# The last of four pairs of feature tiles of each post-sublayer norm on GpSimd instead of VectorE, in a decoder trunk

## The chip, the cores and the metric

The kernel runs on one core of a Trainium2 chip. The metric is device time in microseconds (us) of one execution. Engines are named as the profile names them: PE is TensorE's matmuls, PEld its loads of weights, DVE is VectorE, ACT ScalarE, POOL GpSimd, SP the engine that issues most DMAs.

## What is computed

One inference step of a trunk of four layers, for a prompt of 256 tokens and 8 samples of one token that share all weights (264 columns together, 1024 features, float32). Layer i has a token mixer (sparse attention, gated recurrence, state-space scan, sparse attention again) and then a squared-ReLU MLP. Around every sublayer stands the same frame:

```python
# Every sub-layer: x <- x + gate(c) * RMSNorm_post(f(RMSNorm_pre(x) * (1 + scale(c)) + shift(c)))
def _rmsnorm(x, g):
    x32 = x.astype(jnp.float32)
    y = x32 * lax.rsqrt(jnp.mean(x32 * x32, axis=-1, keepdims=True) + NORM_EPS)
    return (y * g.astype(jnp.float32)).astype(x.dtype)
...
        xp = xp + gtp_m * _rmsnorm(mp, norm_gains[i, 1])
        hp = _rmsnorm(xp, norm_gains[i, 2]) * (1.0 + scp_f) + shp_f
        xp = xp + gtp_f * _rmsnorm(_sq_relu_mlp(hp, w_mlp_in[i], w_mlp_out[i]), norm_gains[i, 3])
```

## The kernel before

Activations lie feature-major: `xT` (the residual x), `mT` (a sublayer's output) and `hT` (its input) are 128 partitions x 8 tiles of features x 264 columns. A program for each engine is written by hand, with semaphores between them; a `Signal` counts what was given on one. Weights stream through a ring of four slots by SP. Nothing in the order is left to a scheduler: what stands in the code of an engine is its order.

`stage_trunk(l, ...)` is one block of instructions for each layer l: the output projection of the mixer, the norm behind it, the norm ahead of the MLP, the MLP, the norm behind that, and the norm ahead of layer l+1's mixer with its first part (or, in the last layer, the transposes to the output). Two sets of norm signals, s0 and s1, serve the two halves. So `post_dve` and what follows it run eight times: four times with s0, behind a mixer, and four times with s1, behind an MLP.

At each of the eight places the work goes like this. The output's squares are added up over the features on PE by a multiplication with ones (`sum_m`, L419, or L617 in the MLP), and ACT makes the root of it in two steps (`rms_act`, L427 and L428), which writes `rstd`. Meanwhile DVE multiplies `mT` by gain times gate (`coef_post`): the prompt's columns tile by tile (L440), the samples' in one operation (L441). Then, with `rstd`, DVE multiplies pairs of tiles by the root (L446, in place) and adds them to x (L455), four pairs, each of 2 tiles x 264 = 528 columns; the multiplication of the next pair stands ahead of the addition of this one. Each addition gives `x_done`.

Then comes the norm ahead of the next sublayer. ACT squares each tile as soon as its pair of x is done (`pre_act`, L494 and L495), PE adds the squares up (`rms_pe`, L413), ACT makes the root again (L427, L428). DVE in the meantime prepares `coef_pre` (L463, L464), waits for the last `x_done`, multiplies the samples' columns (L468) and, ahead of an MLP only, makes two of the four mixed blocks of the MLP's first weights (`early`: L702, L705). Then it multiplies x by the root into `hT` (L474), after which ACT (L501) and DVE (L485) scale and shift, and the next sublayer's matmuls start. While PE has nothing to do, it multiplies ones by ones (`keep_clock`, L406): seven times ahead of the squares and six behind them. In the last layer PE transposes x instead (L831), each pair as its `x_done` comes, DVE copies the results from PSUM (L840), four tiles at a time, and SP writes the output.

The first stage (`stage_first`) loads tables of parameters by DMA on ACT's queue, and PE transposes them (L3133) when `tables_in` has counted 13 of them; two more loads, `relb` and `nar` (narrow constants, L3166 and L3167), count on a semaphore of their own, `narrow_in`, that the matmul behind the transposes (L3136) waits for. GpSimd has no work in this kernel but four fills at its start; it takes part in the barriers between blocks.

Of the kernel before, what the change touches and what calls it, by code (L numbers as in the profile page):

```python
# [16 lines left out]
ALU = mybir.AluOpType  # L17
# [144 lines left out]
def hybrid_trunk(nc, a, outs, consts, stop=None):  # L162
# [3 lines left out]
    with ctx:  # L166
# [11 lines left out]
        xT = sb("xT", [128, DT, T])  # L178
        hT = sb("hT", [128, DT, T])
        mT = sb("mT", [128, DT, T])  # L180
# [72 lines left out]
        taken = signal("taken")  # L253
        fetched = [signal(f"fetched{i}") for i in range(4)]
        ada_loaded = [signal(f"ada_loaded{j}") for j in range(3)]
        ada_ready = signal("ada_ready")
# [14 lines left out]
        class NormSignals:  # L271

            def __init__(self, n):
                self.m_squared = signal(f"m_squared{n}")
                self.m_moved = signal(f"m_moved{n}")
                self.m_summed = signal(f"m_summed{n}")
                self.m_rstd = signal(f"m_rstd{n}")
                self.x_done = signal(f"x_done{n}")
                self.x_squared = signal(f"x_squared{n}")
                self.x_summed = signal(f"x_summed{n}")  # L280
                self.x_rstd = signal(f"x_rstd{n}")
                self.x_scaled = signal(f"x_scaled{n}")
                self.h_sample = signal(f"h_sample{n}")
                self.h_act = signal(f"h_act{n}")
                self.h_dve = signal(f"h_dve{n}")
# [137 lines left out]
        def rms_act(act, summed, done, bank):  # L423
# [4 lines left out]
            done.on(nc.scalar.activation(rstd[:, :], rstd[:, :], ACT.Exp, scale=-0.5))  # L428

        def post_dve(v, s, l, which, moved=None):  # L430

# [6 lines left out]
            for t, ready, k in moved or [(t, s.m_moved, 5 + t) for t in range(DT)]:  # L438
                v.wait_ge(ready.sem, ready.at(k))
                nc.vector.tensor_scalar_mul(mT[:, t, 0:SEQ], mT[:, t, 0:SEQ], coef_post[:, t, 0:1])  # L440
            step(nc.vector.tensor_tensor(mT[:, :, SEQ:T], mT[:, :, SEQ:T], coef_post[:, :, 1:C], ALU.mult))  # L441
            v.wait_ge(s.m_rstd.sem, s.m_rstd.at(1))

# [5 lines left out]
            scale(0)  # L449
            for p in range(4):  # L450
                if p < 3:
                    scale(p + 1)
                v.wait_ge(dve_step.sem, dve_step.at(first + p + 1))
                x = xT[:, 2 * p:2 * p + 2, :]
                s.x_done.on(nc.vector.tensor_tensor(x, x, mT[:, 2 * p:2 * p + 2, :], ALU.add))  # L455

        def pre_dve(v, s, l, which, after_post, early=None):
# [7 lines left out]
            if after_post:  # L465
                v.wait_ge(s.x_done.sem, s.x_done.at(4))
            samples = hT[:, :, SEQ:T]
# [20 lines left out]
        def pre_act(act, s, l, which, bank, after_post):  # L488


            for p in range(4):
                if after_post:
                    act.wait_ge(s.x_done.sem, s.x_done.at(p + 1))
                s.x_squared.on(nc.scalar.activation(sq[:, 2 * p, :], xT[:, 2 * p, :], ACT.Square))  # L494
                s.x_squared.on(nc.scalar.activation(sq[:, 2 * p + 1, :], xT[:, 2 * p + 1, :], ACT.Square))  # L495
# [323 lines left out]
        def output_parts(s):  # L819
            ytok = Place(8448 + 12288)(3, D)  # L820

            def pe_part(pe):
                for i in range(3):
                    n = 128 if i < 2 else NB
                    for h in range(2):
                        if i:
                            pe.wait_ge(mm_taken.sem, mm_taken.at(2 * i + h - 1))
                        for t in range(4):
                            if i == 0:
                                pe.wait_ge(s.x_done.sem, s.x_done.at(2 * h + t // 2 + 1))  # L830
                            ins = nc.tensor.transpose(PS[0:n, h, t * 128:(t + 1) * 128],  # L831
                                                      xT[:, 4 * h + t, i * 128:i * 128 + n], ident)
                        mm_ready.on(ins)
# [1270 lines left out]
        def mixer_nsa(l, h):  # L2104
# [7 lines left out]
            return parts, rest  # L2112

        logs, aux_made, copied = signal("logs"), signal("aux_made"), signal("copied")

# [948 lines left out]
        c_in, x_in, wide_in = signal("c_in"), signal("x_in"), signal("wide_in")  # L3064
        tables_in, narrow_in = signal("tables_in"), signal("narrow_in")
        coef_ready, bounds_raised = signal("coef_ready"), signal("bounds_raised")

        def stage_first():
# [30 lines left out]
            with nc.Block() as block:  # L3099
# [13 lines left out]
                def _(pe):  # L3113
# [15 lines left out]
                    rms_pe(pe, s1.x_squared, s1.x_summed, 3)  # L3129
                    pe.wait_ge(tables_in.sem, tables_in.at(16 * 13))  # L3130
                    for n, (i, r, o) in enumerate(spans):
                        pe.wait_ge(mm_taken.sem, mm_taken.at(9 if n < 4 else n + 6))
                        mm_ready.on(nc.tensor.transpose(PS[:, 4 + n % 4, 0:r], rows[0:r, i, :], ident[0:r, 0:r]))  # L3133
                    pe.wait_ge(narrow_in.sem, narrow_in.at(32))
                    o, n = NARROW_AT["by_dist"]
# [26 lines left out]
                def _(act):  # L3162
                    step = stepper(act, act_step)
                    for src, i, r, n in tables:
                        tables_in.on(act.dma_start(rows[r:r + n, i, :], src), 16)
                    narrow_in.on(act.dma_start(relb, a["rel_bias"]), 16)  # L3166
                    narrow_in.on(act.dma_start(nar, consts[1][:, 0:4352]), 16)  # L3167
                    for j, name in enumerate(("ssd_dt_bias", "ssd_a_log", "ssd_d")):
# [90 lines left out]
        def stage_trunk(l, source, mixer):  # L3259
# [10 lines left out]
            with nc.Block() as block:  # L3270
                @block.sync
                def _(sp):
                    proj_sp(sp)
                    mlp_sp(sp)
                    next_sp(sp)

                @block.tensor
                def _(pe):
# [68 lines left out]
```

## Time and profile before

| | |
|---|---|
| median of 3 runs | 2615.28 us (2610.3 to 2617.28) |
| the profiled execution, its own time | 2611.51 us |
| its span, first to last instruction | 2609.7 us |
| mean granted clock of TensorE | 0.934 |
| PE busy | 2445.3 us, 94% |
| PEld busy | 2071.7 us, 79% |
| DVE busy | 1322.4 us, 51% |
| ACT busy | 740.4 us, 28% |
| POOL busy | 0.2 us |

All rows below are from this one execution; times are us from the start of its span. PE's matmuls are pipelined and the ends of their rows are modelled. A row of the timeline may merge several instructions of one kind that follow each other (x2, x8); the number in its brackets is how long the engine had been idle before it, with what ended the idle time.

### The profile page before, as it was taken

Reading aid. Unit: us, or ns where it says so; the run is one execution under the profiler, and the core shown is the slowest. Engines: PE = TensorE matmul, PEld = TensorE weight load, DVE = VectorE, ACT = ScalarE, POOL = GpSimd, SP = SyncE. Lnnn points to the kernel's source line nnn. Section 1 sums busy time; section 2 is a strip of 40 time slices with the busy share of each in tenths; the row PEclk is TensorE's granted clock in tenths of the full one; section 3 lists DMA queues with packets and bytes.
Section 4 is the critical chain, followed back from the end, with each engine's and each line's share of the span. In section 5 each row is a group of like instructions: output and inputs, shape, how many; then the busy total and the mean of one; then the engine's idle time right before and its main releaser. Section 6 shows DMA issues by size and latency. Waiting matters only on the chain. (4 is left out here: it accounts for less than half of the span.)

```text
span 2609.7 us, 45644 instructions
## 1 busy us (share of the span) xinstructions
PE 2445.3 (94%) x19266; PEld 2071.7 (79%) x19266; DVE 1322.4 (51%) x2361; ACT 740.4 (28%) x1781; POOL 0.2 (0%) x4
## 2 busy tenths in 40 slices
PE   8989988999999888999999896999999899989998
PEld 6668865699986766999888664899985787648998
DVE  2257374366542464555443395165540874535665
ACT  1125373211022342210232393121011454522200
POOL 0000000000000000000000000000000000000000
PEclk8999798999999978999999856999999997889999
DMA  9997617867633325676333252666653875093440
GB/s 345 289 247 162 207 41 222 294 227 268 250 129 129 97 73 193 237 278 240 131 129 131 66 162 73 217 255 247 252 179 79 178 202 156 27 322 137 168 176 30
DMA packets 287344, 472.73 MB, mean 181 GB/s; under 512 B 14956, under 2 KB 105149, under 8 KB 286662
## 3 DMA queue, kind: packets, MB, share of 16 engines
q1 hardware_dynamic: 272370, 456.04, 53.6%
q10 hardware_dynamic: 14770, 13.76, 1.7%
q8 instruction: 153, 2.51, 0.4%
q14 instruction: 51, 0.42, 0.0%
HBM read 448.72 MB, written 38.04 MB: 187 GB/s over the span
## 5 line engine op out<-in xcount | busy, mean ns | idle before, releaser
L598 PE MATMUL PS<-hT,ring 128*128 128x132 f32 x2048 | 250.3, 277 | 6.1 <-DVE hT L723 4.2
L598 PEld LDWEIGHTS PS<-hT,ring 128*128 128x128 f32 x2048 | 238.3, 190 | 12.6 <-issue 11.8
L598 PE MATMUL PS<-mT,arena 128*128 128x132 f32 x1536 | 185.3, 276 | 0.0
L598 PEld LDWEIGHTS PS<-mT,arena 128*128 128x128 f32 x1536 | 179.1, 190 | 0.0
L2624 PE MATMUL PS<-hT,ring 128*128 128x264 f32 x768 | 172.7, 386 | 0.3 <-DVE hT L480 0.3
L2624 PEld LDWEIGHTS PS<-hT,ring 128*128 128x128 f32 x768 | 145.1, 190 | 25.1 <-issue 0.6
L735 DVE TENSOR_TENSOR arena<-arena,PS 128x264 f32<-128x264 f32 x224 | 89.7, 427 | 129.4 <-PE PS L598 128.3
L682 ACT ACTIVATE arena<-arena 128x528 f32<-128x528 f32 x64 | 41.1, 642 | 311.8 <-DVE arena L735 311.8
L1443 DVE COPY arena<-PS 64x512 f32<-64x512 f32 (+1 forms) x160 | 94.2, 588 | 68.8 <-PE PS L1317 67.7
L598 PE MATMUL PS<-arena,ring 128*128 128x132 f32 x1024 | 127.5, 278 | 0.0
L598 PE MATMUL PS<-mT,ring 128*128 128x132 f32 x1024 | 125.7, 276 | 0.0
L598 PE MATMUL PS<-hT,arena 128*128 128x132 f32 x1024 | 125.7, 276 | 0.0
L598 PEld LDWEIGHTS PS<-arena,ring 128*128 128x128 f32 x1024 | 120.1, 190 | 3.6 <-issue 3.6
L598 PEld LDWEIGHTS PS<-hT,arena 128*128 128x128 f32 x1024 | 120.5, 190 | 0.3
L598 PEld LDWEIGHTS PS<-mT,ring 128*128 128x128 f32 x1024 | 120.2, 190 | 0.0
L1462 ACT ACTIVATE arena<-PS 64x512 f32<-64x512 f32 (+1 forms) x160 | 82.9, 518 | 125.3 <-PE PS L1317 124.3
L2077 PE MATMUL PS<-hT,ring 128*128 128x264 f32 x384 | 92.1, 396 | 13.4 <-PEq L2524 9.9
L687 ACT ACTIVATE hT<-PS 128x264 f32<-128x264 f32 x8 | 3.1, 390 | 351.2 <-PE PS L598 351.2
L2077 PEld LDWEIGHTS PS<-hT,ring 128*128 128x128 f32 x384 | 74.8, 195 | 27.4 <-issue 14.2
L440 DVE TENSOR_SCALAR mT<-mT,coef_post 128x256 f32<-128x256 f32 x64 | 20.1, 351 | 150.8 <-ACT mT L394 150.7
L2139 PE MATMUL PS<-hT,ring 128*128 128x264 f32 x384 | 85.9, 386 | 0.3 <-DVE hT L480 0.3
L1051 PE MATMUL PS<-ring,hT 128*128 128x512 f32 x192 | 84.7, 596 | 1.3 <-DMA ring<-in_nsa_w_in 1.3
(473 smaller groups left out, 4423.4 us busy)
## 6 DMA issues: line engine op xcount, KB each, us to landing
arena<-in_w_ada SPq DMA_DIRECT2D x36, 2048.0 KB, 12.1
ring<-in_w_mlp_in SPq DMA_DIRECT2D x32, 2048.0 KB, 8.6
ring<-in_w_mlp_out SPq DMA_DIRECT2D x32, 2048.0 KB, 8.4
ring<-in_w_ada SPq DMA_DIRECT2D x12, 2048.0 KB, 16.8
ring<-in_ssd_w_in SPq DMA_DIRECT2D x12, 2048.0 KB, 8.0
ring<-in_nsa_w_in SPq DMA_DIRECT2D x10, 2048.0 KB, 9.4
arena<-in_cache_nsa_kv SPq DMA_DIRECT2D x64, 256.0 KB, 11.1
ring<-in_cache_nsa_kv SPq DMA_DIRECT2D x64, 256.0 KB, 7.7
```

Of the source, the lines that this page charges most:

```text
L440: nc.vector.tensor_scalar_mul(mT[:, t, 0:SEQ], mT[:, t, 0:SEQ], coef_post[:, t, 0:1])
L598: ins = nc.tensor.matmul(PS[:, bank, at:at + HALF], lhs[:, k, p * 128:(p + 1) * 128], rhs[:, k, :], start=opens and k == 0, stop=closes an ...
L682: step(nc.scalar.activation(x, x, ACT.Relu))
L687: mlp_copied.on(nc.scalar.activation(n1, both(0), ACT.Copy))
L735: mlp_sums.on(nc.vector.tensor_tensor(dst, x, y, ALU.add))
L1051: ins = nc.tensor.matmul(PS[:, n % 4, :], hT[:, k, m * 128:(m + 1) * 128], w[:, k, :], start=k == 0, stop=k == 7)
L1443: ins = nc.vector.tensor_copy(dst, src)
L1462: ins = nc.scalar.activation(dst, src, ACT.Copy)
L2077: ins = nc.tensor.matmul(PS[:, 4 * h + m, 0:T], w[:, k, m * 128:(m + 1) * 128], src[:, 8 * d + k, :], start=d == 0 and k == 0, stop=d == d ...
L2139: ins = nc.tensor.matmul(PS[:, n % 4, 0:T], w[:, k, m * 128:(m + 1) * 128], hT[:, k, :], start=k == 0, stop=k == 7)
L2624: ins = nc.tensor.matmul(PS[:, n % 4, 0:T], w[:, k, m * 128:(m + 1) * 128], hT[:, k, :], start=k == 0, stop=k == 7)
```

## The change

In each of the eight places the fourth pair of tiles (tiles 6 and 7) of `mT` is multiplied by the root and added to x by GpSimd, in a new function `post_pool`; VectorE does the first three pairs. GpSimd waits for a new semaphore, `m_weighted`, that VectorE raises when the weights of the samples are in, and for the root; between its two instructions it waits for the first. What waited for the fourth `x_done` now waits for `x_done_pool`: ScalarE's squares of tiles 6 and 7, VectorE's L468, and PE's transposes of tiles 6 and 7 at the end. To have the three semaphores for this, two of `fetched`, one of `ada_loaded` and `narrow_in` go; the two loads of `narrow_in` are counted on `tables_in`, so that the transposes of the parameter tables wait for them too.

```diff
-        fetched = [signal(f"fetched{i}") for i in range(4)]
-        ada_loaded = [signal(f"ada_loaded{j}") for j in range(3)]
+        fetched = [signal(f"fetched{i}") for i in range(2)]
+        ada_loaded = [signal(f"ada_loaded{j}") for j in range(2)]
...
+                self.x_done_pool = signal(f"x_done_pool{n}")
...
+        def post_pool(gp, s, n):
+
+
+            m, x = mT[:, 6:8, :], xT[:, 6:8, :]
+            gp.wait_ge(m_weighted.sem, m_weighted.at(n + 1))
+            gp.wait_ge(s.m_rstd.sem, s.m_rstd.at(1))
+            pool_step.on(nc.gpsimd.tensor_tensor(m, m, bc(rstd[:, :], 1, 2), ALU.mult))
+            gp.wait_ge(pool_step.sem, pool_step.at(n + 1))
+            s.x_done_pool.on(nc.gpsimd.tensor_tensor(x, x, m, ALU.add))
+
         def post_dve(v, s, l, which, moved=None):
...
             step(nc.vector.tensor_tensor(mT[:, :, SEQ:T], mT[:, :, SEQ:T], coef_post[:, :, 1:C], ALU.mult))
+            v.sem_inc(m_weighted.sem, 1)
+            m_weighted.given += 1
             v.wait_ge(s.m_rstd.sem, s.m_rstd.at(1))
...
-            for p in range(4):
-                if p < 3:
+            for p in range(3):
+                if p < 2:
                     scale(p + 1)
...
             if after_post:
-                v.wait_ge(s.x_done.sem, s.x_done.at(4))
+                v.wait_ge(s.x_done.sem, s.x_done.at(3))
+                v.wait_ge(s.x_done_pool.sem, s.x_done_pool.at(1))
...
             for p in range(4):
-                if after_post:
+                if after_post and p < 3:
                     act.wait_ge(s.x_done.sem, s.x_done.at(p + 1))
+                elif after_post:
+                    act.wait_ge(s.x_done_pool.sem, s.x_done_pool.at(1))
...
-                            if i == 0:
+                            if i == 0 and 4 * h + t < 6:
                                 pe.wait_ge(s.x_done.sem, s.x_done.at(2 * h + t // 2 + 1))
+                            elif i == 0:
+                                pe.wait_ge(s.x_done_pool.sem, s.x_done_pool.at(1))
...
-                    pe.wait_ge(tables_in.sem, tables_in.at(16 * 13))
+                    pe.wait_ge(tables_in.sem, tables_in.at(16 * 15))
...
-                    pe.wait_ge(narrow_in.sem, narrow_in.at(32))
...
-                    narrow_in.on(act.dma_start(relb, a["rel_bias"]), 16)
-                    narrow_in.on(act.dma_start(nar, consts[1][:, 0:4352]), 16)
+                    tables_in.on(act.dma_start(relb, a["rel_bias"]), 16)
+                    tables_in.on(act.dma_start(nar, consts[1][:, 0:4352]), 16)
...
+                @block.gpsimd
+                def _(gp):
+                    post_pool(gp, s0, 0)
+                    post_pool(gp, s1, 1)
```

DVE's instructions behind the mixer of layer 0, before, from the weights of the samples to the first multiplication into `hT` (in brackets the semaphores waited for):

```order
L441 TENSOR_TENSOR mT<-mT,coef_post 128x8x8
L446 TENSOR_TENSOR mT<-mT,rstd 128x528 [waits m_rstd0,dve_step]
L446 TENSOR_TENSOR mT<-mT,rstd 128x528
L455 TENSOR_TENSOR xT<-xT,mT 128x528 [waits dve_step]
L446 TENSOR_TENSOR mT<-mT,rstd 128x528
L455 TENSOR_TENSOR xT<-xT,mT 128x528 [waits dve_step]
L446 TENSOR_TENSOR mT<-mT,rstd 128x528
L455 TENSOR_TENSOR xT<-xT,mT 128x528 [waits dve_step] x2
L463 TENSOR_SCALAR coef_pre<-mod 128x72
L464 TENSOR_TENSOR coef_pre<-coef_pre,par 128x72 [waits dve_step]
L468 TENSOR_TENSOR hT<-xT,coef_pre 128x8x8 [waits x_done0,dve_step]
```

The same stretch on DVE after the change (line numbers are those of the changed kernel):

```order
L452 TENSOR_TENSOR mT<-mT,coef_post 128x8x8
L459 TENSOR_TENSOR mT<-mT,rstd 128x528 [waits dve_step,m_rstd0]
L459 TENSOR_TENSOR mT<-mT,rstd 128x528
L468 TENSOR_TENSOR xT<-xT,mT 128x528 [waits dve_step]
L459 TENSOR_TENSOR mT<-mT,rstd 128x528
L468 TENSOR_TENSOR xT<-xT,mT 128x528 [waits dve_step] x2
L476 TENSOR_SCALAR coef_pre<-mod 128x72
L477 TENSOR_TENSOR coef_pre<-coef_pre,par 128x72 [waits dve_step]
L482 TENSOR_TENSOR hT<-xT,coef_pre 128x8x8 [waits x_done_pool0,x_done0,dve_step]
```

One multiplication and one addition are gone from the row, and the samples' operation waits for GpSimd too. GpSimd, which had no rows here, has in each layer's block:

```order
L437 TENSOR_TENSOR mT<-mT,rstd 128x528 [waits m_rstd0,m_weighted]
L439 TENSOR_TENSOR xT<-xT,mT 128x528 [waits pool_step]
L437 TENSOR_TENSOR mT<-mT,rstd 128x528 [waits m_rstd1,m_weighted]
L439 TENSOR_TENSOR xT<-xT,mT 128x528 [waits pool_step]
L3288 UNCONDITIONAL_BRANCH
```

The first two stand behind the mixer, the next two behind the MLP; the second pair waits in the queue for most of the block.

## Rows read from the trace of the kernel before

**Rows 1.** The page: busy time by engine (share, instructions), and the chain's shares.

```profile
PE 2445.3 (94%) x19266; PEld 2071.7 (79%) x19266; DVE 1322.4 (51%) x2361; ACT 740.4 (28%) x1781; POOL 0.2 (0%) x4
...
PE 9%; DVE 1%; ACT 0%; issue 0%; DVEq 0%
```

**Rows 2.** One line, L446: duration ns min/median/max, first and last start, form.

```profile
L446 DVE TENSOR_TENSOR mT<-mT,rstd x32: 698/702/710, 505.6 to 2598.1; 128x528 f32<-128x528 f32 x32
```

**Rows 3.** Timeline, middle place of layer 0: start, length, engine, line, operation [idle before].

```profile
505.55 1.33 DVE L446 TENSOR_TENSOR mT<-mT,rstd 128x528 f32<-128x528 f32 x2 [1.04 <-ACT rstd L428]
506.80 0.70 DVE L455 TENSOR_TENSOR xT<-xT,mT 128x528 f32<-128x528 f32 x1
...
508.03 0.70 DVE L455 TENSOR_TENSOR xT<-xT,mT 128x528 f32<-128x528 f32 x1
508.65 0.70 DVE L446 TENSOR_TENSOR mT<-mT,rstd 128x528 f32<-128x528 f32 x1
...
509.25 0.74 PEld L413 LDWEIGHTS PS<-arena,ones 128*128 128x128 f32 x4 [0.49 <-ACT arena L494]
509.27 1.32 DVE L455 TENSOR_TENSOR xT<-xT,mT 128x528 f32<-128x528 f32 x2
510.01 0.42 ACT L494 ACTIVATE arena<-xT 128x264 f32<-128x264 f32 x1 [0.50 <-DVE xT L455]
...
510.48 1.63 PEld L413 LDWEIGHTS PS<-arena,ones 128*128 128x128 f32 x8 [0.50 <-ACT arena L494]
...
511.00 0.22 DVE L468 TENSOR_TENSOR hT<-xT,coef_pre 128x64 f32<-128x64 f32 x1
...
512.52 1.23 DVE L705 TENSOR_TENSOR ring<-ring 128x1024 f32<-128x1024 f32 x1
...
513.08 0.42 ACT L428 ACTIVATE rstd<-rstd 128x264 f32<-128x264 f32 x1
513.66 0.69 DVE L474 TENSOR_TENSOR hT<-xT,rstd 128x512 f32<-128x512 f32 x1
```

**Rows 4.** L474: idle time before it by releaser (us, times); then one mixer place.

```profile
L474 DVE TENSOR_TENSOR hT<-xT,rstd x28: 682/686/694, 513.7 to 2386.7; 128x512 f32<-128x512 f32 x28
...
  ACT rstd L428: 7.1, 3
...
758.56 0.69 DVE L474 TENSOR_TENSOR hT<-xT,rstd 128x512 f32<-128x512 f32 x1 [2.38 <-ACT rstd L428]
```

**Rows 5.** Timeline at the end of the program, behind the last MLP.

```profile
2595.01 1.33 DVE L446 TENSOR_TENSOR mT<-mT,rstd 128x528 f32<-128x528 f32 x2 [0.24 <-ACT rstd L428]
...
2598.11 0.70 DVE L446 TENSOR_TENSOR mT<-mT,rstd 128x528 f32<-128x528 f32 x1
...
2598.73 1.32 DVE L455 TENSOR_TENSOR xT<-xT,mT 128x528 f32<-128x528 f32 x2
...
2599.96 1.31 DVE L840 COPY arena<-PS 128x512 f32<-128x512 f32 x2
2600.10 0.20 PEld L831 LDWEIGHTS PS<-wide,xT 128*128 128x128 f32 x2 [0.42 <-DVE xT L455]
```

**Rows 6.** Timeline: GpSimd's work, first of its four fills.

```profile
0.24 0.10 POOL L3332 MEMSET const-float32-0.0<- 128x1 f32 x1 [0.24 <-issue]
```

**Rows 7.** First stage: issue of the narrow table, the transposes; DMA issues with us to landing.

```profile
6.30 0.44 ACTq L3167 DMA_DIRECT2D arena<-const_narrow  x1
...
21.17 0.56 PEld L3133 LDWEIGHTS PS<-wide,arena 128*128 128x128 f32 x4
...
arena<-const_narrow ACTq DMA_DIRECT2D x1, 544.0 KB, 8.2
```

**Rows 8.** Busy us (count) by engine in stretches; PEclk is the granted clock.

```profile
core 0: us, PE busy (x) PEld busy (x) DVE busy (x) ACT busy (x) POOL busy (x), PEclk, DMA share, GB/s
...
507.50:512.40 4.90, 4.23 (x17) 3.01 (x18) 4.80 (x9) 2.84 (x8) 0.00 (x0) 1.00 1.05 405
...
2595.70:2599.10 3.40, 1.70 (x8) 0.78 (x6) 3.40 (x7) 0.00 (x0) 0.00 (x0) 1.00 0.01 2
2599.10:2602.50 3.40, 2.67 (x14) 1.70 (x15) 2.88 (x6) 0.00 (x0) 0.00 (x0) 0.80 0.00 0
```

More of the change, by code:

```diff
@@ L2112, in mixer_nsa @@
             return parts, rest
+        m_weighted = signal("m_weighted")
         logs, aux_made, copied = signal("logs"), signal("aux_made"), signal("copied")
@@ L3064, in hybrid_trunk @@
         c_in, x_in, wide_in = signal("c_in"), signal("x_in"), signal("wide_in")
-        tables_in, narrow_in = signal("tables_in"), signal("narrow_in")
+        tables_in = signal("tables_in")
         coef_ready, bounds_raised = signal("coef_ready"), signal("bounds_raised")
```

## The prediction, made before the change was run

> **What bounds the kernel now.** I read the page's busy shares first, then the chain that ended last, then the stretch around one norm in order of time. TensorE is busy 94% of the span, VectorE 51%, GpSimd not at all, and the chain that ended last lies almost wholly on TensorE [rows 1]. So a change on VectorE counts only where TensorE has nothing else to do. Those places are the norms behind a sublayer: x may not be multiplied again before it is scaled, added, squared, summed, scaled again and shifted. There are eight of them: 32 multiplications by the root of 0.702 us, four at a place [rows 2]. Four are "middle" places (behind a mixer, ahead of the MLP), three are "mixer" places (behind an MLP, ahead of the next mixer), and one is the end (ahead of the output).
>
> The middle place of layer 0 [rows 3]. VectorE starts the first multiplication at 505.55 and then runs eight operations of one pitch, 509.27 - 508.65 = 0.62 us, each 0.70 us long. Call them S0 S1 A0 S2 A1 S3 A2 A3 (S multiplies a pair by the root, A adds it to x). ScalarE squares each pair when its A ends: the third from 510.01. TensorE adds up the squares: eight loads of weights for the last four tiles from 510.48, 1.63 us, so 0.41 us a tile without a gap. From the third pair on it is TensorE's own pace, not VectorE, that sets when the sum is there: the chain runs through A2, not through A3. Then come the second root (its end 513.08 + 0.42 = 513.50) and VectorE's L474 at 513.66. In a middle place VectorE has its own chain beside it: L468 at 511.00, two preparations of weights, the last from 512.52 for 1.23 us, so until 513.75. That is as late as the root. L474 waited for the root at three places only, the mixer places, with 2.38 us idle [rows 4].
>
> **What the change does to each part.**
>
> 1. S3 and A3 leave VectorE: 2 x 0.62 us at each of eight places. If nothing else is touched, A2 starts at 508.65 instead of 509.27. Its pair could be squared 0.62 us earlier, but TensorE began the second pair's two tiles at 509.25 [rows 3] and needs 0.82 us for them, so the third pair starts at 510.07 instead of 510.48: **0.41 us gained** on the sum. In a middle place VectorE's own chain ends 1.24 us earlier, at 512.51, ahead of the root at 513.09; L474 gains 0.41 and the 0.05 us by which it followed the root later there than at a mixer place. Seven places: 7 x 0.41 + 4 x 0.05 = 3.1 us. At the end of the program the last pair is transposed from 2600.10 and the copy that waited for it followed [rows 5]. With A2 ended 0.62 us earlier, tiles 4 to 7 need 0.88 us from 2598.86: done 2599.74 instead of 2600.54, of which VectorE's copies leave 0.6. Sum: **-3.7 us**.
>
> 2. GpSimd makes the pair: two operations of 128x528 at each place, in its own queue with nothing behind them. Behind its results wait ScalarE (squares of the last pair, and behind them the root and the shifts), VectorE (L468 and behind it the two preparations and L474), and at the end TensorE. No row shows GpSimd computing at this width; it has four fills of one column, 0.10 us each [rows 6]. Bounds: 0.70 us (VectorE's own price) and 1.4 us, twice that. I take 1.25 us, near VectorE's 1.23 us for 1024 columns [rows 3], since an engine without a second fast reader would read the two inputs of 528 columns one behind the other. By the Trainium skill, "GPSIMD Engine Reference", section "Elementwise — side-by-side cycle accounting", it is 1.96 times VectorE's time at 2048 columns; by that alone it would be an estimated 1.38 us. No run here shows it yet. Undisturbed, the pair is ready at 505.55 + 0.1 + 2 x 1.25 + 0.1 = 508.25. It is needed for a square that must be done when TensorE reaches tile 6 (510.07 + 0.82 = 510.89), so from about 510.45: over 2 us to spare. Each operation could last 2.3 us and still cost nothing.
>
> 3. The new wait and the semaphore. VectorE adds one to a semaphore behind L441 (the samples' weights). Its idle time ahead of S0 is 1.04 us at a middle place [rows 3] and 0.24 us at the others [rows 5], of which 0.13 lies before the root is there. Cost 0 to 0.1 us at four places; I take 0.
>
> 4. The merged wait in the first stage. The transposes of the parameter rows, from 21.17 us, now also wait for the table of narrow constants. It was issued at 6.30 and landed 8.2 us later, at 14.5 [rows 7]. The cover is the sum of squares ahead of the transposes; 6.7 us to spare. Cost 0. The three semaphores taken away are waited for nowhere.
>
> **What the two engines do to each other** is the term that decides. Every one of VectorE's six remaining operations reads two tensors of SBUF, and so do both of GpSimd's; all start from the same root at the same moment. ScalarE squares x beside VectorE's additions and neither is longer for it: all 32 multiplications lie between 698 and 710 ns [rows 2]. That speaks for free running, but shows ScalarE, not GpSimd. If the two share a way to SBUF and an operation holds it to its end, the work of both is in line: 6 x 0.62 + 2 x 1.25 = 6.2 us where eight operations took 4.96. Who goes first decides what it costs.
>
> - In turns: S0, GpSimd, S1, GpSimd, A0, S2, A1, A2. A1 ends at 511.23, A2 at 511.85 (before: 508.73, 509.97). TensorE starts the second pair 0.52 us behind A1, at 511.75, and the third at 512.57 instead of 510.48: **+2.1 us**. At the end A2 ends at 2601.31 and 0.9 us of transposes follow: +1.7. Sum 7 x 2.1 + 1.7 = **+16.4 us**.
> - VectorE first, since its next operation stands ready when one ends: A2 is 0.62 us early, GpSimd starts at 509.27 and its pair is done at 511.9. Tile 6 is summed from 512.35 instead of 511.30: +1.05 at a mixer place, about +1.0 at a middle one (VectorE's chain, held at L468, ends 514.7), +1.3 at the end. Sum 4.0 + 3.1 + 1.3 = **+8.4 us**.
>
> With GpSimd at 0.70 us the two are +7.6 and about 0, with 1.4 us +18.5 and +10.5.
>
> I forecast that they are in line, between the two orders: **+12.4 us**. The reason is the place more than the price: each pair of GpSimd operations meets a row of VectorE operations without a gap [rows 3], so any exclusion, whichever engine wins, falls on the chain. The skill has a rule that speaks against this change: "SBUF — State Buffer", section "Who interferes with whom", says a VectorE instruction with two SBUF inputs contends with a GpSimd instruction that reads SBUF, the second blocking until the first is finished. By it the two sums above hold, without it the -3.7; no row here shows it yet.
>
> **The rivals.**
>
> - *Free running.* GpSimd and VectorE don't disturb each other, or only GpSimd is longer and stays inside its 2 us to spare. Then -3.7 us. For it: ScalarE beside VectorE, and the wide margin. Against it: no row has GpSimd in it. Time 2615.3 - 3.7 = 2611.6.
> - *The clock falls too.* With the turns, TensorE is empty from 507.5 to 510.5, between its filling multiplications and the first square; today it is 4.23 of 4.90 us busy there at a granted clock of 1.00. At the end of the program a stretch of 3.4 us in which it was busy 1.70 us is followed by one with a mean of 0.80, part of it at 1.2 GHz instead of 2.4 [rows 8]. At 0.80 over 3.4 us 1.4 us are at half speed, 0.7 lost; at most 1.7 us if all is. Seven places: 5 to 12 us on top of 16.4, so some +25 us: 2640.
>
> **How the numbers follow.** The sums are against the profiled execution (span 2609.7, its time 2611.5); the median of the three runs is 3.8 us higher, and the same differences are put on it: 2615.3 + 12.4 = 2627.7, rounded to **2627.5 us**. Chances: in line 0.52, free running 0.38, clock too 0.08, something else 0.02. A measurement of this kernel tells about 0.3%, 7.8 us, from no change. No case gains that much: faster 0.02. Slower: most of the first case (0.44; the rest has a quick GpSimd or VectorE going first), the clock and half of the unknown, 0.54. Within 0.3%: 0.44. The range reaches from the free case less 3 us of spread, 2608, to the turns with GpSimd at 1.4 us and the same spread, 2637; beyond it lies mainly the clock case.
>
> **What would show it.** Right: at eight places GpSimd operations over 1.3 us long or starting only when a VectorE operation ends, VectorE operations with pitches of 1.8 us in the row S0 to A2, L474 one to two us later after S0 than the 8.11 us of today. Free running: the six operations at pitches of 0.62, GpSimd done before A2, the third pair's sum 0.4 us earlier. Clock: a granted clock under 1.00 in the 13 us behind a place. The forecast is wrong above all if reading two tensors on both engines is no conflict, or if GpSimd's stretch of waiting fits into its own 2 us.

## The result

The changed kernel takes 2640.77 us (median of 4 runs, 2637.74 to 2643.12), the kernel before 2612.84 (4 runs, 2610.3 to 2617.28): a ratio of 1.010, interval 1.0084 to 1.0115, so **slower by 22 to 30 us**. Measured twice more, it was 1.0071 (1.0049 to 1.0093) and 1.0101 (1.0082 to 1.0119). The sign is the forecast's, and so is the cause, two engines in line; the size is not. 2640.8 lies above the range's 2637, and where I wrote 12.4 us it was about 20 at the eight places alone. One of the six runs of the kernel called *idle pair beside* below took 6151.68 us and is in no time or ratio given here.

The page of the changed kernel, busy shares and the chain, as [rows 1] of before:

```profile
PE 2453.3 (93%) x19266; PEld 2080.0 (79%) x19266; DVE 1331.2 (50%) x2345; ACT 740.1 (28%) x1781; POOL 27.4 (1%) x20
...
PE 9%; DVE 1%; ACT 0%; issue 0%
```

VectorE has 16 instructions fewer (2361 to 2345) and yet is busy for 9 us longer. The groups by line say which (us busy and mean ns of one; line 459 is 446 of before, 468 is 455):

```profile
L459 DVE TENSOR_TENSOR mT<-mT,rstd 128x528 f32<-128x528 f32 x24 | 25.0, 1070 | 4.5 <-ACT rstd L429 4.5
...
L468 DVE TENSOR_TENSOR xT<-xT,mT 128x528 f32<-128x528 f32 x24 | 24.9, 1062 | 0.0
```

```profile
L437 POOL TENSOR_TENSOR mT<-mT,rstd 128x528 f32<-128x528 f32 x8 | 14.0, 1755 | 2600.3 <-ACT rstd L429 2600.3
L439 POOL TENSOR_TENSOR xT<-xT,mT 128x528 f32<-128x528 f32 x8 | 13.1, 1639 | 0.6
```

Where a multiplication by the root had a mean of 0.702 us [rows 2], it now has 1.07. That is no general slowness. The timeline of the first place, which answers to [rows 3], shows it to be two operations at each place (start, length, engine, line, operation, idle time before):

```profile
512.39 2.43 DVE L459 TENSOR_TENSOR mT<-mT,rstd 128x528 f32<-128x528 f32 x2 [0.97 <-ACT rstd L429]
512.51 1.75 POOL L437 TENSOR_TENSOR mT<-mT,rstd 128x528 f32<-128x528 f32 x1 [512.06 <-ACT rstd L429]
514.34 1.64 POOL L439 TENSOR_TENSOR xT<-xT,mT 128x528 f32<-128x528 f32 x1
514.75 1.79 DVE L468 TENSOR_TENSOR xT<-xT,mT 128x528 f32<-128x528 f32 x1
516.47 0.70 DVE L459 TENSOR_TENSOR mT<-mT,rstd 128x528 f32<-128x528 f32 x1
516.58 0.42 ACT L510 ACTIVATE arena<-xT 128x264 f32<-128x264 f32 x1 [4.22 <-DVE xT L468]
...
517.05 5.62 PE L414 MATMUL PS<-arena,ones 128*128 128x264 f32 x16 [2.65 <-ACT arena L510]
517.08 1.31 DVE L468 TENSOR_TENSOR xT<-xT,mT 128x528 f32<-128x528 f32 x2
...
518.29 3.96 PEld L414 LDWEIGHTS PS<-arena,ones 128*128 128x128 f32 x12 [0.49 <-ACT arena L510]
...
523.67 0.69 DVE L488 TENSOR_TENSOR hT<-xT,rstd 128x512 f32<-128x512 f32 x1 [2.12 <-ACT rstd L429]
```

S0 and GpSimd's multiplication start 0.12 us apart. GpSimd's ends at 514.26; only then does S1, ready since 513.0, run: it ends at 514.82, 0.56 us later. GpSimd's addition then ends at 515.98, and A0, begun at 514.75, again 0.56 us behind it, at 516.54. After that the pitches are 0.62 us as before. So they take turns: S0, GpSimd, S1, GpSimd, A0. (A row's length counts from its start, so GpSimd's rows, and S1's and A0's, hold their waiting as well as their work.) A0 ends 4.15 us behind the start of S0 instead of 1.95. TensorE, which now has 2.65 us without work, begins the squares 2.2 us late; from the second pair on it has no more gaps, as it had none from the third pair on before. From S0 to the first multiplication into hT it is 11.28 us, where it was 8.11.

Part of the 11.28 is the clock. In the same stretch the granted clock, which had been 1.00, is 0.85, and twelve loads take 3.96 us, where at the second place they take 2.52:

```profile
core 0: us, PE busy (x) PEld busy (x) DVE busy (x) ACT busy (x) POOL busy (x), PEclk, DMA share, GB/s
512.40:523.70 11.30, 8.65 (x32) 6.57 (x31) 9.04 (x12) 3.63 (x10) 3.39 (x2) 0.85 1.04 398
```

```profile
766.34 2.52 PEld L414 LDWEIGHTS PS<-arena,ones 128*128 128x128 f32 x12 [0.49 <-ACT arena L510]
...
770.36 0.69 DVE L488 TENSOR_TENSOR hT<-xT,rstd 128x512 f32<-128x512 f32 x1 [3.27 <-ACT rstd L429]
```

That second place (a mixer place, S0 at 760.45) takes 9.91 us at a clock of 1.00, where it took 8.06 [rows 4]. Over the seven places ahead of the output the stretch is 11.28, 9.91, 9.85, 11.60, 11.51, 9.91 and 11.39 us, where it was 8.11 or 8.05; the first, fourth, fifth and seventh have a fall of the clock in them. Sum 18.9 us, and 1.2 more from the last S0 to the end: **20.1 us**. The span grew by 31.2. Of the rest, 6.8 us lie ahead of the first place, where nothing of the norm has run, and 4.0 in the recurrence of layer 1.

### The profile page after: what moved, and what is told of

Its sections match the earlier page's. It is cut to its first block and busy times, and to the rows that moved or that the text cites. A ratio compares the mean times of both kernels' runs of the same rounds, so it can differ in the third digit from the quotient of the medians.

```text
span 2640.9 us, 45654 instructions
## 1 busy us (share of the span) xinstructions
PE 2453.3 (93%) x19266; PEld 2080.0 (79%) x19266; DVE 1331.2 (50%) x2345; ACT 740.1 (28%) x1781; POOL 27.4 (1%) x20
## 5 line engine op out<-in xcount | busy, mean ns | idle before, releaser
L614 PEld LDWEIGHTS PS<-hT,ring 128*128 128x128 f32 x2048 | 238.3, 190 | 12.1 <-issue 11.4
L451 DVE TENSOR_SCALAR mT<-mT,coef_post 128x256 f32<-128x256 f32 x64 | 20.1, 352 | 153.7 <-ACT mT L395 153.6
```

The lines of the kernel that those rows point to most:

```text
L614: ins = nc.tensor.matmul(PS[:, bank, at:at + HALF], lhs[:, k, p * 128:(p + 1) * 128], rhs[:, k, :], start=opens and k == 0, stop=closes an ...
```

## The experiments

Two theories stood after that. *Turns*: an operation of either engine holds a way to SBUF that both need when VectorE reads two tensors of SBUF and GpSimd reads too, and the other waits for its end. *Waiting*: GpSimd's result is late, and who waits for it is late. Besides, the 6.8 and 4.0 us outside the places had to be given to the change or to the spread of the runs. The table has, for each kernel, the stretch from S0 to the first multiplication into hT in us, the sum of all eight places against the kernel before (the end, from the last S0 to the end of the span, included), and the ratio to the kernel before measured beside it. All come from the kernel's profile and its runs.

| kernel | middle places | mixer places | eight places, us | ratio (95% interval) |
|---|---|---|---|---|
| before | 8.11 | 8.05 to 8.06 | 0 | 1 |
| changed | 9.85, with fall 11.3 to 11.5 | 9.91, with fall 11.6 | +20.1 | 1.010 (1.0084 to 1.0115) |
| changed, second time | 9.84, with fall 11.0 to 11.5 | 9.91, with fall 11.5 to 11.6 | +21.2 | 1.0071 (1.0049 to 1.0093) |
| changed, third time | 9.85, with fall 11.3 to 11.5 | 9.91 to 9.92, with fall 11.6 | +20.1 | 1.0101 (1.0082 to 1.0119) |
| merged wait only | 8.11 | 8.05 to 8.06 | 0.0 | 0.9988 (0.9973 to 1.0003) |
| idle pair beside | 10.27, with fall 10.9 to 11.2 | 10.19, with fall 11.3 to 11.4 | +22.4 | 1.0076 (1.0053 to 1.0100) |
| only writes beside | 8.10 to 8.11 | 8.05 | 0.0 | 0.9991 (0.9973 to 1.0010) |
| late pair | 9.50 to 9.86 | 9.45 to 9.46 | +12.0 | 1.0052 (1.0034 to 1.0070) |
| more filling | 9.85 | 9.91 to 9.92 | +14.0 | 1.0057 (1.0040 to 1.0074) |
| through PSUM | 7.61 to 7.62 | 7.68 | -5.0 | 0.9980 (0.9964 to 0.9996) |
| through PSUM, second time | 7.62 | 7.69 to 7.70 | -4.9 | 0.9995 (0.9980 to 1.0010) |
| PSUM without GpSimd | 8.08 to 8.09 | 8.03 | -0.3 | 0.9999 (0.9981 to 1.0017) |
| GpSimd behind mixers only | 9.84, with fall 11.0 to 11.5 | 8.05 to 8.06 | +11.9 | 1.0039 (1.0019 to 1.0058) |
| GpSimd behind MLPs only | 8.11 to 8.12 | 9.91, with fall 11.1 | +8.7 | 1.0035 (1.0015 to 1.0054) |

### The changed kernel again

> The changed kernel once more, nothing edited, to see what of its +31 us of span repeats. Its first profile reached the first multiplication by the root behind the mixer of layer 0 at 512.39 us, where the kernel before had 505.55, and nothing of the norm had run by then. If this 6.8 us belongs to the change (a wait, GpSimd's code), the second profile has it again within 1 us. If it is the spread of TensorE's granted clock in the attention, it moves by several us either way. At the eight places both expect the same as in the first profile: the second and third VectorE operations 1.8 us long, GpSimd's 1.75 and 1.64 us. Time 2637 to 2644.

The median was 2634.32 us (10 runs, 2620.25 to 2642.79), under the 2637 to 2644 I expected, and the first S0 came at 504.32 instead of 512.39. The 6.8 us do not belong to the change. Over the first 500 us the granted clock was 0.90 in the first profile of the changed kernel, 0.92 in the second and 0.93 in the third (0.91 in the kernel before). The third time the first S0 came at 502.93; over all kernels of this study it lies between 502.9 and 514.0, although none edits the attention. GpSimd's operations were 1755 and 1640 ns again. The recurrence ahead of the third place, though, took 269.5 us again.

> The changed kernel a third time, on the same chip as e3_again. By the eight places it loses 20 to 21 us: 2632 to 2636 beside 2614. If the first measurement's 28 us were the truth: 2641.

2639.11 us (5 runs, 2633.82 to 2640.32) beside 2613.44: above the 2632 to 2636 I expected, and nearer the first measurement than the second. The places gave 20.1 us again.

### The merged wait alone

```diff
# kernel before
-                    pe.wait_ge(tables_in.sem, tables_in.at(16 * 13))
+                    pe.wait_ge(tables_in.sem, tables_in.at(16 * 15))
...
-                    pe.wait_ge(narrow_in.sem, narrow_in.at(32))
```

> The kernel before with only the merged wait of the first stage (the transposes of the parameter tables wait for 15 loads instead of 13) and without the three semaphores; GpSimd does nothing and VectorE makes all four pairs. If the merged wait is covered, as forecast: the time of the kernel before, 2610 to 2617, and the transposes at 21.2 us as before. If it is what makes the first stage late: 3 to 7 us more.

2612.25 us, ratio 0.9988 with 1 in the interval: no cost. In the changed kernel too the transposes were not late; their first load starts at 20.52 us, where it started at 21.17 [rows 7]:

```profile
20.52 0.56 PEld L3152 LDWEIGHTS PS<-wide,arena 128*128 128x128 f32 x4
```

### An idle pair beside VectorE, reading and then only writing

```diff
# merged wait only
+                @block.gpsimd
+                def _(gp):
+                    for n, s in enumerate((s0, s1)):
+                        gp.wait_ge(s.m_rstd.sem, s.m_rstd.at(1))
+                        pool_step.on(nc.gpsimd.tensor_tensor(spare[:, :], wide[:, 0:512], wide[:, 512:1024], ALU.mult))
+                        gp.wait_ge(pool_step.sem, pool_step.at(2 * n + 1))
+                        pool_step.on(nc.gpsimd.tensor_tensor(spare[:, :], wide[:, 0:512], wide[:, 512:1024], ALU.add))
+                        gp.wait_ge(pool_step.sem, pool_step.at(2 * n + 2))
```

> VectorE makes all four pairs, as before the change; GpSimd, on the same signal of the root, multiplies and then adds two constant tiles of 128x512 from SBUF into a tile that nobody reads, so nobody waits for it. (With the merged wait of e1_wait_only.) If the two engines are in line for SBUF (in turns): VectorE's second and third operation at each place are 1.8 us long, its fourth addition ends 2.4 us later than before, and the time is 19 to 28 us above the kernel before: 2632 to 2642. If the loss came from waiting for GpSimd's result, or from the order of the pairs: VectorE's eight operations keep their pitch of 0.62 us and the time is 2610 to 2617.

Nobody reads `spare`, VectorE makes all four pairs, and the kernel is slower all the same: ratio 1.0076, interval 1.0053 to 1.0100, median 2638.96 of five runs. Timeline of its first place:

```profile
513.98 1.26 POOL L3281 TENSOR_TENSOR spare<-wide 128x512 f32<-128x512 f32 x1 [513.52 <-ACT rstd L429]
514.00 3.48 DVE L447 TENSOR_TENSOR mT<-mT,rstd 128x528 f32<-128x528 f32 x2 [1.04 <-ACT rstd L429]
515.32 1.61 POOL L3283 TENSOR_TENSOR spare<-wide 128x512 f32<-128x512 f32 x1
517.41 0.70 DVE L456 TENSOR_TENSOR xT<-xT,mT 128x528 f32<-128x528 f32 x1
```

Here GpSimd is first by 0.02 us, as at all four middle places. S0 and S1 together take 3.48 us instead of 1.33; they are what waits here, one behind each of GpSimd's two, and A0 has its 0.70 us. At the mixer places and at the end S0 is first by 0.04 us, and the second and third operation wait (1.77 and 1.76 us long), as I had expected of all eight. Waiting for a result is ruled out, since there is none. So is a quarrel over one tensor: GpSimd reads `wide` here, which VectorE's row does not touch. The same with fills in place of the two operations:

```diff
# idle pair beside
-                        pool_step.on(nc.gpsimd.tensor_tensor(spare[:, :], wide[:, 0:512], wide[:, 512:1024], ALU.mult))
+                        pool_step.on(nc.gpsimd.memset(spare[:, :], 1.0))
...
-                        pool_step.on(nc.gpsimd.tensor_tensor(spare[:, :], wide[:, 0:512], wide[:, 512:1024], ALU.add))
+                        pool_step.on(nc.gpsimd.memset(spare[:, :], 0.0))
```

> As e5_beside, but GpSimd only writes: two fills of a tile of 128x512 in place of the multiplication and the addition; nobody waits for them. If it is reading by both engines that collides: VectorE's eight operations keep 0.62 us of pitch, and the time is that of the kernel before, 2607 to 2618. If any work of GpSimd at this point holds VectorE: its second operation is longer by what the fill takes.

```profile
504.43 0.53 POOL L3281 MEMSET spare<- 128x512 f32 x1 [503.99 <-ACT rstd L429]
504.49 1.32 DVE L447 TENSOR_TENSOR mT<-mT,rstd 128x528 f32<-128x528 f32 x2 [1.04 <-ACT rstd L429]
505.02 0.53 POOL L3283 MEMSET spare<- 128x512 f32 x1
505.73 0.70 DVE L456 TENSOR_TENSOR xT<-xT,mT 128x528 f32<-128x528 f32 x1
```

VectorE's row is as if GpSimd weren't there: S0 and S1 in 1.32 us, ratio 0.9991. In these two runs writing by GpSimd beside VectorE's reading of two tensors is free; reading is not.

### VectorE with one tensor from SBUF

```diff
# changed kernel
             step(nc.scalar.activation(rstd[:, :], PS[:, bank, 0:T], ACT.Ln, bias=eps[:, :], scale=1.0 / D))
+            if root is not None:
+                done.on(nc.scalar.activation(PS[:, root, 0:T], rstd[:, :], ACT.Exp, scale=-0.5))
...
-            gp.wait_ge(s.m_rstd.sem, s.m_rstd.at(1))
+            gp.wait_ge(s.m_rstd.sem, s.m_rstd.at(2))
...
+            def scaled(p):
+                return PS[:, 4 + 2 * p:6 + 2 * p, 0:T] if p < 2 else mT[:, 2 * p:2 * p + 2, :]
...
-                dve_step.on(nc.vector.tensor_tensor(m, m, bc(rstd[:, :], 1, 2), ALU.mult))
+                dve_step.on(nc.vector.tensor_tensor(scaled(p), m, bc(PS[:, 0 if which == 1 else 2, 0:T], 1, 2), ALU.mult))
...
-                s.x_done.on(nc.vector.tensor_tensor(x, x, mT[:, 2 * p:2 * p + 2, :], ALU.add))
+                s.x_done.on(nc.vector.tensor_tensor(x, x, scaled(p), ALU.add))
```

> The changed kernel, but VectorE reads only one tensor from SBUF in its first operations: ScalarE writes the root to PSUM too (for GpSimd to SBUF, one step later), VectorE multiplies pairs 0 and 1 into PSUM and adds them from there; pair 2 is multiplied in place in SBUF with the root from PSUM and added as before. GpSimd does the fourth pair as in the change. If two SBUF inputs on VectorE are what collides with GpSimd: VectorE's pitches return to 0.62 to 0.70 us, GpSimd's operations fall to 1.25 us each, x_done of the fourth pair comes at about 3 us behind the root, and the time is 2607 to 2616, at or below the kernel before. If GpSimd's work harms VectorE whatever VectorE reads, or the loss has another cause: 2630 to 2645.

First place, timeline:

```profile
508.85 1.33 DVE L464 TENSOR_TENSOR PS<-mT,PS 128x528 f32<-128x528 f32 x2 [0.94 <-ACT PS L430]
509.31 1.31 POOL L439 TENSOR_TENSOR mT<-mT,rstd 128x528 f32<-128x528 f32 x1 [508.86 <-ACT rstd L431]
510.09 0.70 DVE L473 TENSOR_TENSOR xT<-xT,PS 128x528 f32<-128x528 f32 x1
510.70 1.31 POOL L441 TENSOR_TENSOR xT<-xT,mT 128x528 f32<-128x528 f32 x1
510.70 0.70 DVE L464 TENSOR_TENSOR mT<-mT,PS 128x528 f32<-128x528 f32 x1
...
512.53 2.52 PEld L414 LDWEIGHTS PS<-arena,ones 128*128 128x128 f32 x12 [0.49 <-ACT arena L515]
...
516.47 0.69 DVE L493 TENSOR_TENSOR hT<-xT,rstd 128x512 f32<-128x512 f32 x1 [0.68 <-ACT rstd L431]
```

Both engines run through each other undisturbed. VectorE's pitches are 0.61 to 0.62 us, and GpSimd's two operations fall from 1.75 and 1.64 us to 1.31 each, its price where nothing holds it. (A2 still reads two tensors of SBUF; it starts 3.08 us behind S0, less than 0.1 us before GpSimd ends.) The fourth pair is there at 512.01, 3.2 us behind S0. The stretch is 7.62 us, 0.49 less than before, as the forecast's free case has it (0.41 plus the little by which a middle place lagged). So the fault was the shared reading, not the moving of the pair.

The edit also lets GpSimd start later, 0.46 us behind S0 instead of 0.12. That alone doesn't help. In the kernel with GpSimd behind the mixers only (below), which has all its operands in SBUF, GpSimd happened to start 0.45 us behind S0 at one place, and S1 and A0 waited as ever:

```profile
2384.88 2.43 DVE L459 TENSOR_TENSOR mT<-mT,rstd 128x528 f32<-128x528 f32 x2 [0.97 <-ACT rstd L429]
2385.33 1.41 POOL L437 TENSOR_TENSOR mT<-mT,rstd 128x528 f32<-128x528 f32 x1 [685.15 <-ACT rstd L429]
2386.82 1.64 POOL L439 TENSOR_TENSOR xT<-xT,mT 128x528 f32<-128x528 f32 x1
2387.23 1.79 DVE L469 TENSOR_TENSOR xT<-xT,mT 128x528 f32<-128x528 f32 x1
```

In time the gain stays small: the ratio is 0.9980 (0.9964 to 0.9996). The same kernel was measured a second time:

> e3_psum once more, to see whether it is below the kernel before for good. By the places of its first profile (seven times 0.4 to 0.5 us, and 1.9 us at the end) it is 5 us below: a ratio of 0.998 with an interval under 1. If that was the spread of the runs: 1.000.

Now the ratio was 0.9995 (0.9980 to 1.0010), 2612.25 us over 12 runs. The places say -5 us, 0.2%; the runs can't tell it from none. By these runs it is as fast as the kernel before, and perhaps a few us faster.

Is it PSUM that helps? The same kernel with all four pairs on VectorE:

> e3_psum without GpSimd: VectorE makes all four pairs, the first two through PSUM, the last two in place in SBUF with the root from PSUM. (With the merged wait.) If the 0.4 to 0.5 us that e3_psum gains at each place come from the fourth pair moved away: here the stretch is 8.1 us again and the time 2607 to 2618. If they come from PSUM: 7.6 us here too.

2614.29 us, ratio 0.9999, stretch 8.08 us. The gain at the places comes from the pair moved away.

### The pair after VectorE's row

```diff
# changed kernel
             gp.wait_ge(s.m_rstd.sem, s.m_rstd.at(1))
+            gp.wait_ge(s.x_done.sem, s.x_done.at(3))
```

> The changed kernel, but GpSimd also waits for VectorE's third addition (x_done 3), so the two hardly run side by side. If an operation holds the way to SBUF and they take turns: VectorE's six operations have a pitch of 0.62 us again; GpSimd's two last 1.3 us each, as in e3_psum, and end about 6.7 us behind the first multiplication; the stretch from there to the first multiplication into hT is 9.2 us (before 8.1, changed kernel 9.9, or 11.4 where the clock falls), the clock doesn't fall in it, and the time is 2618 to 2626, better than the changed kernel although GpSimd starts 3.7 us later. If GpSimd's result is simply too late in the changed kernel: later still, 11 us or more, over 2640.

```profile
513.06 1.33 DVE L460 TENSOR_TENSOR mT<-mT,rstd 128x528 f32<-128x528 f32 x2 [0.97 <-ACT rstd L429]
514.31 0.70 DVE L469 TENSOR_TENSOR xT<-xT,mT 128x528 f32<-128x528 f32 x1
...
517.04 1.37 POOL L438 TENSOR_TENSOR mT<-mT,rstd 128x528 f32<-128x528 f32 x1 [516.59 <-DVE xT L469]
...
518.49 1.30 POOL L440 TENSOR_TENSOR xT<-xT,mT 128x528 f32<-128x528 f32 x1
519.82 0.42 ACT L511 ACTIVATE arena<-xT 128x264 f32<-128x264 f32 x1 [2.17 <-POOL xT L440]
```

GpSimd starts 3.98 us behind S0 instead of 0.12, 3.9 us later than in the changed kernel, and yet the kernel is no slower than the changed one: its ratio to the kernel before is 1.0052. Six of the seven stretches are 9.45 to 9.52 us, against 9.85 to 9.91 without a fall in the changed kernel (I had expected 9.2); the seventh is 9.86, where VectorE's samples' operation starts 0.49 us behind GpSimd's addition and not 0.13, for a reason I don't know. None has a fall of the clock. This is also the forecast's second order, VectorE first, made on purpose. It costs 1.4 us a place (1.75 at the seventh, 1.85 at the end), where I had put 1.05: GpSimd's pair ends at 519.79, 6.7 us behind S0, not 6.35. The time, 2630.18, is over the 2618 to 2626 I expected of it; the ratio's interval, 9 to 18 us, takes in the 12 of the places.

### TensorE kept busy through the turns

```diff
# changed kernel
-                    rms_pe(pe, s0.x_squared, s0.x_summed, 1, 7)
+                    rms_pe(pe, s0.x_squared, s0.x_summed, 1, 12)
...
-                        rms_pe(pe, s1.x_squared, s1.x_summed, 3, 7)
+                        rms_pe(pe, s1.x_squared, s1.x_summed, 3, 12)
```

> The changed kernel with 12 instead of 7 multiplications of ones ahead of the squares, so that TensorE isn't empty while the two engines take turns. If the fall of the granted clock is 1.6 us at the places where it falls: the stretch from the first multiplication by the root to the first one into hT is 9.8 to 9.9 us at all seven places with no half clock in it, and the time is 4 to 8 us below the changed kernel, 2626 to 2632. If the clock there has nothing to do with TensorE's idle time: 11.4 us at four of seven places as before, and no difference.

Its first place, in a window and in the timeline:

```profile
507.30:517.20 9.90, 9.32 (x42) 7.48 (x41) 9.07 (x12) 3.63 (x10) 3.41 (x2) 1.00 1.04 399
```

```profile
506.14 5.34 PE L407 MATMUL PS<-ones 128*128 128x256 f32 x24
...
511.99 4.17 PE L414 MATMUL PS<-arena,ones 128*128 128x264 f32 x16 [0.50 <-ACT arena L510]
...
517.16 0.69 DVE L488 TENSOR_TENSOR hT<-xT,rstd 128x512 f32<-128x512 f32 x1 [0.68 <-ACT rstd L429]
```

The turns are the same (GpSimd's operations 1757 and 1646 ns on the mean), TensorE is idle 0.50 us ahead of the squares instead of 2.65, the clock stays at 1.00, and all seven stretches are 9.85 to 9.92 us. So of the changed kernel's 20.1 us the idle TensorE's clock has 6.3 (18.9 less 12.6 at the seven places), the turns nearly all the rest. The time, 2630.62, is 15 us above the kernel before by its ratio; the places say 14.

### Half of the places

```diff
# changed kernel, GpSimd behind mixers only (behind MLPs only: which == 3, s0's call goes, and pool_step.at(1))
-            for p in range(3):
-                if p < 2:
+            pairs = 3 if which == 1 else 4
+            for p in range(pairs):
+                if p < pairs - 1:
...
-                s.x_done.on(nc.vector.tensor_tensor(x, x, mT[:, 2 * p:2 * p + 2, :], ALU.add))
+                (s.x_done if p < 3 else s.x_done_pool).on(nc.vector.tensor_tensor(x, x, mT[:, 2 * p:2 * p + 2, :], ALU.add))
...
-                    post_pool(gp, s1, 1)
```

> The change at half of its places: GpSimd makes the fourth pair only at the four middle places (behind a mixer); behind the MLPs VectorE makes all four. By turns: 11.3 us from the first multiplication by the root to the first one into hT at middle places where the clock falls and 9.85 where it doesn't, 8.05 at the mixer places, and at the end 14.6. Loss 4 x 1.74 and up to three falls of 1.5: 7 to 12 us. Of the 4 us that the recurrence ahead of the third place took longer in all three profiles of the changed kernel (269.5 instead of 265.3 to 265.5): if they hang on what happens at the first place, they are here too; if on the second, they are gone.

> The other half: GpSimd makes the fourth pair only behind the MLPs; behind the mixers VectorE makes all four. By turns: 9.9 us at the mixer places without a fall of the clock, 11.6 with one, 8.1 at the middle places, 15.9 at the end. Loss 3 x 1.86 + 1.2 and one or two falls of 1.7: 7 to 10 us. Together with e8_mixer_side the places add up to the 20 us of the changed kernel. The recurrence ahead of the third place: 269.5 here if it hangs on the second place, 265.4 if on the first.

1.0039 and 1.0035: 10 and 9 us, which the places (11.9 and 8.7) account for. They add: 20.6 us by the places, 19 by the ratios. But 0.75 of the 11.9 us is not GpSimd's. They lie at the end, where VectorE makes all four pairs in this kernel as it did before, and where I had expected 14.6 us; it took 15.42 instead of 14.67. VectorE's row is the same, and TensorE's next loads start 5.69 us behind S0 in both kernels. But the low clock came 0.5 us earlier and lay over all of them; eight loads took 1.57 us:

```profile
2612.34 1.57 PEld L850 LDWEIGHTS PS<-wide,xT 128*128 128x128 f32 x8 [0.40 <-DVE arena L859]
```

where before they took 0.42 and 0.72:

```profile
2600.70 0.42 PEld L831 LDWEIGHTS PS<-wide,xT 128*128 128x128 f32 x4 [0.40 <-DVE arena L840]
2601.33 0.72 PEld L831 LDWEIGHTS PS<-wide,xT 128*128 128x128 f32 x4 [0.20 <-DVE arena L840]
```

So a figure for the end can hold some 0.75 us of the clock's luck.

The recurrence's stretch settled on neither side: 268.2 us in the one, 266.4 in the other. Over all kernels it is 263.7 to 269.6 us; the three profiles of the changed kernel and the idle pair's have the longest (269.4 to 269.6), but 268.2 and 267.9 stand in kernels without a fall there or without GpSimd. In the kernel before, one of its rows of matmuls, 64 loads from 920.1, ran at a clock of 1.00; in the changed kernel the same row ran at 0.72:

```profile
920.10:928.00 7.90, 7.41 (x64) 7.22 (x64) 7.48 (x12) 5.79 (x15) 0.00 (x0) 1.00 0.01 2
```

```profile
931.50:942.60 11.10, 10.31 (x64) 10.12 (x64) 8.17 (x13) 3.54 (x9) 0.00 (x0) 0.72 0.01 1
```

These 2.9 us are TensorE's clock, in a stretch of which 44 to 58 us have low clock in every kernel. Why it lies over that row in all three profiles of the changed kernel **stays open**; that the places before shift it is a guess.

## Why the prediction was right and wrong

**What bounds the kernel** held. The stretch of the norm is on the path: at the middle places without a fall TensorE began the squares 2.2 us late, and 1.74 us of it reached the first multiplication into hT.

**Part 1, the gain.** Right as a mechanism, and to be seen only where nothing collides: through PSUM the middle places are 0.49 us shorter and the mixer places 0.37, where I had 0.46 and 0.41. The end is 1.9 us shorter, not 0.6. VectorE's first copy starts 3.70 us behind S0 instead of 4.95, so 1.25 us are the two operations gone from the row, and I had counted half of them. The other 0.7 us are TensorE's clock and no merit of the change: over 2599.10 to 2604.80 it was 0.70 in the kernel before, over the same 20 loads of the kernel through PSUM (2602.35 to 2606.40) 1.00. They are in the -5.0 us of the table too.

**Part 2, GpSimd's price.** I took 1.25 us between 0.70 and 1.4; with nothing to hold it, it is 1.31. By the Trainium skill, "GPSIMD Engine Reference", section "Elementwise — side-by-side cycle accounting", GpSimd takes 1.96 times VectorE's time at 2048 columns; by that it would be an estimated 1.38 us. The runs show 1.31 to 0.70, 1.87 times, at 528 columns. Part of the 1.75 and 1.64 us that the changed kernel's rows give is waiting: 0.45 and 0.33 us. (My sums at 1.4 us are 0.3 too low: two operations longer by 0.15 us at eight places make 2.4, so 18.8 and 10.8; the range's 2637 stays.)

**Parts 3 and 4**, the added semaphore and the merged wait, cost nothing, as forecast: S0 follows the root no later (0.24 us idle ahead of it in [rows 5], less in the changed kernel), and the merged wait alone is at 0.9988.

**The two engines in line** was right. By the Trainium skill, "SBUF — State Buffer", section "Who interferes with whom", a VectorE instruction with two SBUF inputs contends with a GpSimd instruction that reads SBUF, not with one that only writes it. The runs agree in both: VectorE's two SBUF inputs collide with reads of GpSimd (idle pair beside, +22.4 us at the places), not with its writes (0.0). They also don't collide where one of VectorE's inputs comes from PSUM. **The step that failed** is the middle I took between two orders, 12.4 us between 8.4 and 16.4. VectorE does not go first because its next operation stands ready: at every place the two alternate, and I should have let the order "in turns" stand alone. For that order I had +2.1 us a place and +1.7 at the end, 16.4 in all. Measured without the clock it is +1.74 and +1.86, and 1.2 at the end: about 14. A little less, because the turns are shorter than I took them: S1 ends 0.56 us behind GpSimd where I had 0.62, GpSimd's addition 1.16 behind S1 where I had 1.25, and A2 ends 6.01 us behind S0 where the forecast has 6.30. (At the end the clock's luck is in it too.)

**The clock** was the second mis-sized term, in its chance, not its price. I wrote the case down with 5 to 12 us and gave it 0.08. It happened in four places of seven, five the second time and four the third, and cost 6.3 us, some 1.6 us a place, inside the 0.7 to 1.7 I had put. The idle time of 3.0 us that I had worked out (2.65 measured) should have made it part of the main case, as it came from the same turns. 14 and 6.3 make 20 us, 2635 on the forecast's own base, inside the range, as the second measurement's 2634.3 is. The other two, 26 and 28 us above the kernel before, exceed the 20 us of the places by 6 to 8, and so lie above the range. Of the 28, the profile puts 6.8 us ahead of the first place, which did not come back, and 4.0 in the recurrence, which came back each time and whose cause stays open.

## What to carry over

In these kernels work moved to GpSimd beside a busy VectorE was free only where GpSimd didn't read SBUF while VectorE read two tensors from it. Look at the operands of both before the lengths: an operand in PSUM on VectorE's side took the collision away, at no cost in its own pace. When two engines take turns, count also what stands idle behind them: a TensorE left idle for 2.65 us paid again with its clock at four or five places of seven, and filling it won that part back. And before a gain or a loss at one stretch is put down to a change, compare the granted clock of the stretch on both sides.

## What the runs showed of the hardware that I had not expected

- The turns are strict. With VectorE's next operation ready, GpSimd's waiting one still went in between, for each of its 16 operations in the changed kernel (GpSimd's lengths differ by at most 7 ns over eight places).
- GpSimd's rows include its waiting: the same operation is 1755 ns long behind VectorE and 1305 where VectorE takes one operand from PSUM. VectorE's rows do so too: 1809 ns for S1 instead of 702.
- VectorE's pace with an operand in PSUM and the result there is that of SBUF: two multiplications of 528 columns in 1.33 us either way.
- GpSimd's first multiplication, 35 us behind the two instructions MODIFY_POOL_CONFIG in its queue (477.3 us), was no longer than the seven others: 1752 to 1759 ns. Whether a cost of starting was hidden in the 35 us, no run shows.
